# Latent turns inside an attention, rotary queries inside a projection, and a group's leaving in pieces, in a two-block transformer kernel

## What is computed

```
qk = silu(dwconv3(p[..., OFF_MQ:OFF_MV], conv_w, conv_b))
k  = to_mlstm_heads(qk[..., MLSTM_WIDTH:]) * (MLSTM_HEAD_DIM ** -0.5)
d  = rmsnorm(diff_attend(q, k_all, v_all, lam), g_norm) * (1 - lam_init)     # per head of 128
```

```
q, k, v, g_gqa, cq, ckv, kr, g_mla = split(h @ w_in)        # cq, ckv: 512 wide, kr: 64
qm  = (rms_norm(cq, cq_gain) @ w_uq).reshape(B, S, 8, 192)  # 128 plain + 64 rotary
kvm = (rms_norm(ckv, ckv_gain) @ w_ukv).reshape(B, S, 8, 256)
q_rope, kr = apply_rope(q_rope), apply_rope(kr)             # latent tokens only
o_a = block_attention(q, k, v)                              # gqa
o_b = block_attention([q_nope, q_rope], [k_nope, kr], v_mla)
x = x + gate * ([o_a * silu(g_gqa), o_b * silu(g_mla)] @ w_out)
```

## Time and profile before

| | |
|---|---|
| three runs | 3328.53, 3328.86, 3336.1 us; median 3328.86 us |
| the profiled execution | 3333.35 us, of which the span of the core's work is 3331.6 us |
| mean granted TensorE clock | 0.956 |
| PE busy | 3042.3 us, 91% of the span |
| weight loads (PEld) | 2528.0 us, 76%, beside PE |
| DVE busy | 2154.6 us, 65% |
| ACT busy | 1255.5 us, 38% |
| POOL busy | 187.1 us, 6% |
| HBM | 571.72 MB read, 176 GB/s over the span |

### The profile page before, as it was taken

One profiled execution on the slowest core, in us unless ns is written; L12 is line 12 of the kernel. 1 busy time (PEld: TensorE's weight loads), 2 busy tenths in 40 slices (PEclk: granted clock), 3 DMA queues, 4 the chain that ended last, 5 costly groups with the idle time before them and its releaser, 6 DMA issues. The chain is left out here.

```text
span 3331.6 us, 42537 instructions
## 1 busy us (share of the span) xinstructions
PE 3042.3 (91%) x16441; PEld 2528.0 (76%) x16441; DVE 2154.6 (65%) x3112; ACT 1255.5 (38%) x2011; POOL 187.1 (6%) x224
## 2 busy tenths in 40 slices
PE   5999879897789999999998998998899989998997
PEld 2587658786679999998887887786757878886666
DVE  5767545756777879896875679545834644674345
ACT  6631233422344444444334322214234224344243
POOL 1000000001000111110001000000010000000000
PEclk9999889997899999999998999998999999998999
DMA  8876124660377777776784556540512644681323
GB/s 266 278 248 232 53 78 134 220 217 31 134 251 236 238 256 234 230 249 235 265 273 159 160 168 195 179 158 14 173 68 73 205 141 135 212 284 47 114 97 137
DMA packets 255577, 589.24 MB, mean 177 GB/s; under 512 B 21977, under 2 KB 30401, under 8 KB 251024
## 3 DMA queue, kind: packets, MB, share of 16 engines
q1 hardware_dynamic: 246336, 546.64, 49.9%
q0 software_dynamic: 8640, 39.22, 3.3%
q10 hardware_dynamic: 400, 0.66, 0.1%
HBM read 571.72 MB, written 14.72 MB: 176 GB/s over the span
## 5 line engine op out<-in xcount | busy, mean ns | idle before, releaser
L2628 DVE TENSOR_TENSOR w_lo<-raw,w_hi 128x1024 fp32r<-128x1024 f32 (+1 forms) x732 | 886.1, 1226 | 427.4 <-ACT w_hi L2607 417.4
L2607 ACT ACTIVATE w_hi<-raw 128x1024 fp32r<-128x1024 f32 (+1 forms) x732 | 741.6, 1032 | 1061.5 <-PE bank L2678 553.7
L673 DVE SCALAR_TENSOR_TENSOR acc<-raw,sc_t,acc 128x1024 f32<-128x1024 f32 x480 | 603.9, 1286 | 38.3 <-DMA acc<-in_b_ada 32.1
L2686 PE MATMUL bank<-f_hT_hi,w_hi 128*128 128x256 f32 x1408 | 402.2, 286 | 14.1 <-DVE w_lo L2628 14.1
L2676 PE MATMUL bank<-w_hi,l_hT_hi 128*128 128x512 f32 (+1 forms) x1056 | 392.6, 372 | 22.2 <-DVE w_lo L2628 21.9
L2688 PE MATMUL bank<-f_hT_hi,w_lo 128*128 128x256 f32 x1408 | 399.8, 284 | 0.0
L2687 PE MATMUL bank<-f_hT_lo,w_hi 128*128 128x256 f32 x1408 | 399.7, 284 | 0.0
L2678 PE MATMUL bank<-w_hi,l_hT_lo 128*128 128x512 f32 (+1 forms) x1056 | 388.7, 368 | 0.0
L2677 PE MATMUL bank<-w_lo,l_hT_hi 128*128 128x512 f32 (+1 forms) x1056 | 388.7, 368 | 0.0
L2686 PEld LDWEIGHTS bank<-f_hT_hi,w_hi 128*128 128x128 f32 x1408 | 271.6, 193 | 18.4 <-DVE w_lo L2628 16.6
L2687 PEld LDWEIGHTS bank<-f_hT_lo,w_hi 128*128 128x128 f32 x1408 | 271.7, 193 | 0.0
(11 more groups left out here) (434 smaller groups left out, 4720.0 us busy)
## 6 DMA issues: line engine op xcount, KB each, us to landing
raw<-in_w_in SPq DMA_DIRECT2D x240, 512.0 KB, 4.8
raw<-in_w_mod SPq DMA_DIRECT2D x192, 512.0 KB, 5.0
raw<-in_w_ada SPq DMA_DIRECT2D x192, 512.0 KB, 4.6
raw<-in_w_up SPq DMA_DIRECT2D x176, 512.0 KB, 5.0
raw<-in_w_out SPq DMA_DIRECT2D x96, 512.0 KB, 4.9
raw<-in_w_down SPq DMA_DIRECT2D x88, 512.0 KB, 5.3
raw<-in_w_in SPq DMA_DIRECT2D x32, 288.0 KB, 3.2
raw<-in_w_ukv SPq DMA_DIRECT2D x16, 512.0 KB, 4.2
```

The source lines that it names most:

```text
L673: e.scalar_tensor_tensor(acc[a][:, :], raw[s % RAW_SLOTS][:, :], scalar, acc[a][:, :], ALU.mult, ALU.add).then_inc(fma_done, 1)
L2607: e.activation(slot(w_hi[u % SPLIT_SLOTS], g.width), slot(raw[s % RAW_SLOTS], g.width), ACT.Copy).then_inc(hi_ready, 1)
L2628: e.tensor_tensor(slot(w_lo[u % SPLIT_SLOTS], g.width), slot(raw[s % RAW_SLOTS], g.width), slot(w_hi[u % SPLIT_SLOTS], g.width).bitcast(F3 ...
L2686: e.matmul(o, hi[:, kk, c], xh[:, k, 0:n], start=first, stop=False)
```

## The change

**Layers of block 2.** The two `turn` stages and the kr stage are gone. Their work is nine *pieces*: four k-tiles of cq, four of ckv, and kr. Piece n runs inside the first attention, in step 6 + n of 16 (`FIRST = 6`), through bank 1, the keys' bank. In the step, PE does the piece's transposes first, ACT the copy last, and DVE the subtraction last. PE's transposes of a piece wait until DVE's part of the piece before it is through (`lat_lo`), and for the key copy.

The attention ahead of the key projection (the context one in layer 0, the first one in layer 1) also splits the first three units of weights, in steps 10, 12 and 14 on ACT and a step later on DVE (`ahead`).

The rotary stage is gone. The rotation's six parts hang on DVE before consecutive units of the key projection, from the sixth step on behind the last `w_uq_2` group; these three groups leave after three steps (`leave_after = 3`). The transposes of the rotated columns are two more in each `pe_prep` of mla, into the free half of q's bank, and DVE's copy of q is followed by a copy of these. `gl_pool`, the load of the gates, is issued at the start of POOL's part of mla. The F steps of the key projection move from `[(0, 12)]` to `[(2, 11)]`.

**Block 1's second projection.** The leaving of an mk or mq group is cut: DVE does two feature tiles at the leaving, the other two at the next unit; the SiLU is two operations, at the next unit and the one after, and the scaling of mk moves to ACT behind each. `diff_norms` is gone as a side job: its squares with sums move to ACT (eight operations of 128 columns before mo1's unit 5 and eight before unit 7), the reciprocal root is hooked to DVE at mq0's unit 1 and the scaling at its units 2 to 5.

```diff
-                leave = ... else min(at + (1 if g.soon else LEAVE_AFTER), end)
+                leave = ... else min(at + g.leave_after, end)
...
-        def turn(X, tiles, nk, hi, lo, pre=None, scale=None, ahead=None):
...
+        def turn_piece(X, tiles, k, hi, lo, scale):
+            n = n_seen["lat"] = n_seen.get("lat", 0) + 1
+            w = P * len(tiles)
+
+            def pe(e, bank):
+                e.wait_ge(lat_lo, n - 1)
+                for t in range(len(tiles)):
+                    mm = e.transpose(bank[:, P * t:P * t + P], X[:, t, P * k:P * k + P], ident)
+                mm.then_inc(lat_tr, 1)
+
+            def act(e, bank):
+                e.wait_ge(lat_tr, n)
+                e.activation(hi[:, k, 0:w], bank[:, 0:w], ACT.Copy, scale=vecT[:, scale + k:scale + k + 1]).then_inc(lat_hi, 1)
+
+            def dve(e, bank):
+                e.wait_ge(lat_hi, n)
+                e.scalar_tensor_tensor(lo[:, k, 0:w], bank[:, 0:w], vecT[:, scale + k:scale + k + 1],
+                                       hi[:, k, 0:w].bitcast(F32), ALU.mult, ALU.subtract).then_inc(lat_lo, 1)
+
+            return pe, act, dve
+
+        def rows_piece(X, dst):
...
@@ attention: pe_prep, pe, act, dve_qcopy, dve @@
+                if rope is not None:
+                    for n, t in enumerate(qtiles):
+                        mm = e.transpose(q_bank[0:64, P * (nq + n):P * (nq + n) + P], rope[2](h, t), ident)
...
                 for s in range(-3, N + 1):
+                    if s in extra:
+                        e.wait_ge(a_kcopy, kidx(items[min(s + 2, N - 1)][0]) + 1)
+                        extra[s][0](e, k_bank)
...
+                    if s in extra:
+                        extra[s][1](e, k_bank)
+                    for n in range(ahead):
+                        if s == N - 2 * (ahead - n):
+                            fill["act"](e, n)
...
+                last = e.tensor_copy(qT[:, h % 2, 0:nq * P], q_bank[:, 0:nq * P])
+                if rope is not None:
+                    last = e.tensor_copy(rope[0][:, h % 2, 0:nq * P], q_bank[0:64, nq * P:2 * nq * P])
...
+                    if s in extra:
+                        extra[s][2](e, k_bank)
+                    for n in range(ahead):
+                        if s == N - 2 * (ahead - n) + 1:
+                            fill["dve"](e, n)
...
@@ conv_group_qk @@
+            def rest(e):
+                dp(e, g, (2, 3))
+                e.wait_ge(conv_out, 4 * n + 4)
+                e.sem_inc(evac_dve, 1)
+
+            def silu(js):
+                def act(e):
+                    e.wait_ge(conv_out, 4 * n + js.stop)
+                    last = e.activation(dst[:, js, :], dst[:, js, :], ACT.Silu)
+                    if kscale:
+                        chain(e, "act", last)
+                        last = e.activation(dst[:, js, :], dst[:, js, :], ACT.Copy, scale=HD ** -0.5)
+                    last.then_inc(silu_out, 1) if js.stop == 4 else None
+                return act
+
+            g = Group("B", w_in, KT, col, 512, tiles, lhs1, act, lambda e, g: dp(e, g, (0, 1)))
+            g.later = [("dve", 1, rest), ("act", 1, silu(slice(0, 2))), ("act", 2, silu(slice(2, 4)))]
...
+        def diff_squares(t):
+            def act(e):
+                for h in range(HEADS):
+                    last = e.activation(o1[:, 0, HD * h:HD * h + HD], o1[:, t, 1024 + HD * h:1024 + HD * h + HD], ACT.Square,
+                                        accum_out=tiny[:, 8 * t + h:8 * t + h + 1])
+                last.then_inc(diff_sq, 1)
+                e.wait_ge(diff_sq, t + 1)
+            return act
...
+            hook(hooks, "act", at(mo1, 5), diff_squares(0))
+            hook(hooks, "act", at(mo1, 7), diff_squares(1))
+            hook(hooks, "dve", at(mq0, 1), diff_rsqrt)
+            for i in range(4):
+                hook(hooks, "dve", at(mq0, 2 + i), diff_scale(i // 2, 4 * (i % 2)))
...
-              side=(mk1, diff_norms, 1), first=gd_pool, hooks=gates_hooks)
+              first=gd_pool, hooks=gates_hooks)
...
@@ layer() @@
-            stage(**turn(cq, qt, 4, cqT_hi, cqT_lo, scale=V_CQ[l]))
-            stage(**turn(ckv, ALL_TILES, 4, ckT_hi, ckT_lo, scale=V_CKV[l]))
+            pieces = [turn_piece(cq, qt, k_, cqT_hi, cqT_lo, V_CQ[l]) for k_ in range(4)]
+            pieces += [turn_piece(ckv, ALL_TILES, k_, ckT_hi, ckT_lo, V_CKV[l]) for k_ in range(4)]
+            pieces.append(rows_piece(kr, krT))
+            FIRST = 6
...
-            gqa(LAT_TILES, ALL_TILES)
+            gqa(LAT_TILES, ALL_TILES, {FIRST + n: p for n, p in enumerate(pieces)}, 3 if last else 0)
             if not last:
-                gqa(CTX_TILES, CTX_TILES)
+                gqa(CTX_TILES, CTX_TILES, {}, 3)
...
-            stage(pe=kr_pe, act=kr_act)
...
+            for g in gs[0:3]:
+                g.leave_after = 3
...
+                hook(hooks, "dve", main_units(steps, 1, uq_group), qr_ready)
+                for n, part in enumerate(parts):
+                    hook(hooks, "dve", main_units(steps, 1 + n, uq_group), part)
...
-                gemms(gs, sums_l1[1][0:1], hosts=[(0, 12)])
+                gemms(gs, sums_l1[1][0:1], hosts=[(2, 11)], hooks=qr_hooks)
...
             def gl_gate(e):
+                gl_pool(e)
                 e.wait_ge(aux_landed, need2)
...
-            stage(dve=qr_dve, pe=qr_pe, act=qr_act, pool=gl_pool)
```

179 lines of the change are left out of this document (70 added, 109 removed).

## The result

| | before | after |
|---|---|---|
| median of the runs | 3328.7 us (4 runs) | 3355.53 us (3347.48 to 3356.86, 4 runs) |
| ratio | | 1.0072, 95% interval 1.0051 to 1.0093 |
| span of the profiled execution | 3331.6 us | 3355.0 us |

What follows compares the result with a forecast made beforehand. PE was taken to bound the matmul stages and the attention. Layer 0 +2.7, layer 1 -3.5 and second projection -11 gave -11.8 us; with the clock's +9, -2.8: 3326 us, range 3313 to 3342.

Steps and rivals of the forecast that it cites:

- waits in the piece steps: First attentions: PE and DVE take turns, 5.06 us a step instead of 2.39; +21.2 us in layer 0, +19.2 in layer 1.
- clock in the piece steps: First attentions: PE's pauses of 2.1 us lower its clock; 4.5 us a layer, +9 together, bounds 0 and 47.
- splits ahead, context attention: Layer 0's context attention: splitting three weight units early lengthens it by +3.0 us, bounds 0 and 6.9.
- key projection: Units split ahead shorten it: -2.0 us in layer 0, where DVE falls into debt, and -6.7 in layer 1.
- second projection: Block 1's second projection: cutting the groups' leaving and moving the norm removes PE's waits; -11 us, bounds -4 and -17.
- rival 4: First attentions: the pieces hide and cost their transposes only; -42 us, 3287 us, chance 0.05.
- four stalls of layer 0's key projection: PE waits for w_lo at units 5, 7, 9 and 11, by 2.0, 2.8, 1.9 and 1.9 us.
- It goes: -12.0 and -9.2: Rotary stage between key projection and mla: its removal saves 12.0 us in layer 0 and 9.2 in layer 1.
- the attention gets two more transposes a head: mla: 0.22 us a head on PE and 0.2 at each start; +3.7 us in layer 0, +1.9 in layer 1.
- under the scores: mla: DVE's second copy of 0.4 us a head is hidden while PE does the scores.
- rival 1: First attentions: the clock holds through pauses of 2.1 us; sum -11.8 us, 3317 us, chance 0.14.
- rival 2: First attentions, steps 7 to 14: the half clock feeds itself; +47 us instead of +9, 3364 us, chance 0.10.

Runs made afterwards that it cites:

- e13_fillpieces: The changed kernel with 16 unread identity transposes on PE ahead of each piece but the first, during PE's wait: 3335.94 us, ratio 1.0015.
- e1_first: The changed kernel with each piece's copy first in ACT's step and its split first in DVE's step, instead of last: 3289.78 us, ratio 0.9877.
- e10_leave5: e1_first with layer 0's three w_uq_2 groups leaving after five steps again instead of three: 3287.91 us, ratio 0.9861.
- e15_turnfill: e12_best with identity transposes among one-column matmuls of two sum turns, and 12 behind the one after layer 0's key projection: 3277.23 us, ratio 0.9833.
- e4_rotstage: The changed kernel with the rotary stage put back and its hooks, extra mla transposes and leave_after = 3 removed: 3341.27 us, ratio 1.0036.
- e12_best: e1_first with five-step leaving in layer 0, identity transposes during gate waits and ahead of layer 1's mla, and split waits for q's copies: 3281.24 us.
- e6_warm: e1_first with 12 (layer 0) or 16 (layer 1) unread identity transposes at the end of each key projection: 3287.37 us, ratio 0.9862.
- e14_fillentry: The changed kernel with 8 unread identity transposes at the entry of layer 0's second mla attention: 3347.14 us, ratio 1.0044.
- e9_again: The changed kernel timed and profiled once more, with nothing altered: 3354.54 us, ratio 1.0057 against the kernel before.
- e11_gates: e1_first with 60 (layer 0) and 40 (layer 1) unread identity transposes while PE waits for the gates to be stored: 3294.39 us, ratio 0.9887.
- e8_noahead: e1_first without the splits ahead; the key projections' first units are split when their phase begins: 3299.55 us, ratio 0.9902.
- e2_stages: The changed kernel with the pieces undone: both turn stages and a kr stage again stand ahead of the first attention: 3307.51 us, ratio 0.9931.
- e7_pool: e1_first with the rotary parts on POOL instead of DVE, each operation awaited: 3294.6 us, ratio 0.9884.
- e3_qsplit: The changed kernel with one more semaphore in mla: only a score's second matmul waits for the copy of the rotary rows: 3348.81 us, ratio 1.0045.
- e5_proj2: The kernel before with only the second projection's part of the change: 3316.61 us, ratio 0.9954.

## Why the prediction was wrong

By its own terms, from the two profiled executions and, for the parting of wait and clock, e13_fillpieces:

| term | forecast | measured |
|---|---|---|
| turn stages | -11.2, -9.0 | -11.1, -8.9 |
| waits in the piece steps | +21.2, +19.2 | +21.2, +19.3 |
| clock in the piece steps | +9 together | +6.7, +9.2 |
| splits ahead, context attention | +3.0 | +0.6 |
| key projection | -2.0, -6.7 | +3.5, -5.6 |
| end of the key projection to mla | -12.0, -9.2 | -12.8, -8.4 |
| mla | +3.7, +1.9 | +16.3, +5.0 |
| second projection | -11 | -14.1 |

The forecast's rows sum to -2.8 (with +0.3 for layer 1's splits), the measured ones to +20.9; the spans differ by 23.4, of which 1.7 lie ahead of the second projection. The parting of waits and clock holds to a microsecond or so: the low clock at the start of layer 1's attention is 8.4 us long in e13_fillpieces and 6.0 in the changed kernel.

**What was right.** The order on the two engines: pauses of 2.2 us for the 2.13 worked out, and the two sums to 0.1 us. Some of that closeness is luck: PE's own terms add up to 2.98 us with half of the 0.33 for q, not 2.93. That the pieces hide (rival 4) was excluded by the rows, and e1_first shows that it took one move in the orders of ACT and DVE to make it true, at 3289.8 us; the rival's own terms give -45 and not -42. The four stalls of layer 0's key projection came as walked: 2.05, 2.85, 1.25 and 1.25 us at units 5, 7, 9 and 11, forecast with 2.0, 2.8, 1.9 and 1.9. The walk had DVE standing for the groups that leave after three steps: it stands 7.08, 2.54 and 3.91 us for PE in the changed kernel, and e10_leave5 shows that this is the cause, since the waits went with the rotary operations left in place. The second projection was right in place and short by 3 us.

**The step that failed** is "It goes: -12.0 and -9.2", taken with "the attention gets two more transposes a head", which stood for all that mla would pay. Its two halves were right: the stretch ahead of mla lost 12.8 and 8.4 us, and at full clock an mla stage of layer 0 costs 106.6 us (e15_turnfill), 3.5 more than before. What was left out is that the rotary stage had also been the place where the low clock behind the key projection was spent, at 0.57, while PE had little to do. e4_rotstage puts the stage back, and mla is at 1.00 in both layers. Without it the stretch ahead of mla shrank to 5.0 and 2.1 us, but the low clock came all the same and fell on an attention in which PE is the bound: 110.9-106.6 = 4.3 us in layer 0 (e12_best against e15_turnfill), 70.8-67.5 = 3.3 in layer 1 (e6_warm). The changed kernel also met it at the entry of the context attention, 119.4-111.5 = 7.9 us (e14_fillentry), where the pause ahead of the first scores had grown from 0.68 to 1.00 us. The forecast had DVE's second copy "under the scores", but at an attention's entry no scores stand ahead of it (the kernel before, then the changed one):

```profile
2511.52 0.67 PE L1014 MATMUL bank<-l_mkT,l_mqT 128*128 128x256 f32 x2 [0.68 <-DVE l_mqT L1093]
2515.25 0.67 PE L1005 MATMUL bank<-l_mkT,l_mqT 128*128 128x256 f32 x2 [1.00 <-DVE l_qrT L1094]
```

The three losses, 15.5 us together, are nearly all of mla's miss of 15.7, and more than half of the whole.

**The term that was mis-sized** is the clock of the piece steps, 15.9 us for the 9 taken; the half clock was put at 4.5 us a layer from block 1's attention, and cost 6.7 and 9.2 in this execution (in e9_again's layer 0 it was 3.3 more). The stage of layer 0's key projection has 5.5 us more than forecast at a clock of 0.94, of which the forecast had allowed 0.6: the same kind, and 3.0 less in e9_again. All in all the forecast had one place for the clock, the piece steps, where the runs show four.

The forecast weighed the Trainium skill's rule on HAM oscillation (TensorE: Matmul & The Clock Gate), which lays the loss of the clock on pauses longer than these, and by which the sum was that of rival 1, 3317 us. Here the measurement decides against it: pauses of 2.2 us with the piece steps cost 15.9 us, and filling them (e13_fillpieces) gave them back. The section of the Trainium skill on a second HAM failure mode, on the same page, has short and frequent pauses do it, and that agrees with the trace.

Rival 2 had the right sign and the wrong place and size: the half clock did not feed itself in the piece steps (0.85 in the mean, not 0.50), it moved on into mla.

**What stays open.** What decides whether the low clock follows a pause isn't shown. Ahead of layer 1's mla a pause of 2.1 us was followed by it in nine profiled executions and not in e11_gates. Filled with 16 transposes it wasn't in any of three (e6_warm, e12_best, e15_turnfill). At the entry of layer 0's second mla attention, with pauses of 0.5 and 1.0 us, it came in the changed kernel (twice), e8_noahead, e11_gates and e13_fillpieces, for some 3 us in e10_leave5, and not in e1_first, e2_stages, e6_warm and e7_pool. With 0.68 us in place of the 1.0 it didn't come in any of six (before, e3_qsplit, e4_rotstage, e5_proj2, e12_best, e15_turnfill). e14_fillentry agrees with a filled pause taking the loss away, but one profiled execution doesn't prove it, since four of the unfilled ones kept their clock too. How much the splits ahead are worth isn't shown either (e8_noahead).

## What to carry to other kernels

When work is slipped into a software-pipelined loop through a buffer that one engine fills and another empties, look where the emptying stands in its engine's order: at the end of a step that starts when the filling engine is done, it puts the two in series; at the front it cost 2.8 and 2.2 us here, a difference of some 65 us for moving two calls. Before a short stage with an idle PE is removed, read the clock of what follows it: the stage may be where the low clock is spent, and its removal can hand that loss to the next stage in which PE is the bound; the price is to be counted there. Where PE has to wait in any case, transposes that nobody reads cost nothing and kept the clock in these runs (pauses of 7.0, 4.7, 2.2 and 2.1 us), as long as they ended before the wait did. The gain needn't last: see what e11_gates had in its mla.

## What the runs showed of the hardware

- A pause of PE of 2.1 us ahead of layer 1's mla was followed by 0.50 on the attention's first microseconds in most profiles (e1_first, 71.9 us, mean clock 0.93). It was not in e11_gates (67.5 us, 1.00), nor was a pause of 1.4 us (e7_pool, 67.6 us, 1.00), nor the pause of 2.1 us filled with 16 transposes (e6_warm, 67.5 us, 1.00).
- The profile shows a run of 32 one-column matmuls as PE busy (3.62 us at full clock), but the granted clock fell to 0.50 within it in e6_warm, e10_leave5 and e12_best. With a transpose of 128 columns behind each second one, and 12 more behind the run, it stayed at 1.00 through it and through mla (e15_turnfill).
- Once low, the clock stayed at 0.50 for 15 us of an attention in which PE was busy without a gap (2517.1 to 2532.2, after), and for 6 us and more behind the first entry (from 2446.9).
- DVE's operations on 1024 columns with two inputs in SBUF (L677) took 1.28 us each, but 1.62 in the mean, up to 1.76, for the ten that ran beside POOL's rotary operations (e7_pool).
- A gain of clock in one stage was not kept by the whole: e11_gates took 2.7 us off layer 0's first attention and, some 240 us later, had 8 us more in its mla than e1_first. Whether the one brought about the other isn't shown, with one profiled execution of each.
